# Ending the first feed-forward part in block products for all eight output tiles

## The reference

```
# first block, last step: x is 512 x 1024, hidden width 2816 = 22 x 128
h = rms_norm(x, norm_ffn_g)
x = x + (silu(h @ w_gate) * (h @ w_up)) @ w_down      # the feed-forward part
x = rms_norm(x, final_g)
# second block, first step
h = rms(x, norm_mix_g_2)
z = h @ w_in_2 + b_in_2                               # gates first, then the projections
```

## Time and profile before

| | |
|---|---|
| median of three runs | 1629.12 us |
| profiled execution | 1627.02 us |
| its span | 1625.3 us |
| PE busy | 1609.5 us, 99% |
| DVE busy | 1085.7 us, 67% |
| ACT busy | 804.6 us, 50% |
| POOL busy | 146.4 us, 9% |
| granted clock of PE, mean | 0.999 |

### The profile page before, as it was taken

The page is one execution under the profiler, slowest core; times in us unless marked ns, Lnnn a source line. Parts: engine busy times, 40 slices in busy tenths (PEclk is TensorE's granted clock), DMA queues, the critical chain, the costliest instruction groups (busy, mean ns, idle before and its releaser), DMA issues. The chain is left out here.

```text
span 1625.3 us, 23389 instructions
## 1 busy us (share of the span) xinstructions
PE 1609.5 (99%) x9266; PEld 1369.7 (84%) x9266; DVE 1085.7 (67%) x1592; ACT 804.6 (50%) x1242; POOL 146.4 (9%) x173
## 2 busy tenths in 40 slices
PE   9999999999999999999999999999999999999999
PEld 7788878888888779999999977777767888998889
DVE  5346755555573458886896896766555688867886
ACT  5344333333453347654654665256685555444453
POOL 0001001112210001000000030313111200000000
PEclk9999999999999999999999999999999999999999
DMA  8653986969756954555556749442213564363225
GB/s 297 244 184 107 246 260 189 313 245 237 222 172 216 257 139 143 182 182 176 179 186 228 246 156 237 157 160 66 66 57 125 150 201 139 117 201 107 86 90 182
DMA packets 83644, 290.32 MB, mean 179 GB/s; under 512 B 9472, under 2 KB 11648, under 8 KB 76560
## 3 DMA queue, kind: packets, MB, share of 16 engines
q1 hardware_dynamic: 76464, 238.46, 42.7%
q0 software_dynamic: 6784, 49.84, 14.5%
q10 hardware_dynamic: 288, 0.54, 0.1%
HBM read 284.58 MB, written 96.50 MB: 234 GB/s over the span
## 5 line engine op out<-in xcount | busy, mean ns | idle before, releaser
L2042 DVE TENSOR_TENSOR WL<-raw,WH 128x1024 fp32r<-128x1024 f32 (+2 forms) x358 | 420.8, 1176 | 220.1 <-ACT WH L1260 206.2
L1260 ACT ACTIVATE WH<-raw 128x1024 fp32r<-128x1024 f32 (+3 forms) x360 | 360.9, 1005 | 257.6 <-PE pst L576 251.2
L576 PE MATMUL pst<-XH,WH 128*128 128x512 f32 x960 | 385.8, 402 | 0.4 <-DVE WL L2042 0.4
L576 PE MATMUL pst<-XH,WL 128*128 128x512 f32 x960 | 374.4, 390 | 0.0
L576 PE MATMUL pst<-XL,WH 128*128 128x512 f32 x960 | 374.0, 390 | 0.0
L576 PEld LDWEIGHTS pst<-XH,WH 128*128 128x128 f32 x960 | 180.2, 188 | 48.0 <-issue 11.7
L576 PEld LDWEIGHTS pst<-XL,WH 128*128 128x128 f32 x960 | 180.4, 188 | 38.2 <-issue 2.6
L576 PEld LDWEIGHTS pst<-XH,WL 128*128 128x128 f32 x960 | 180.2, 188 | 38.3
L576 PE MATMUL pst<-TH,WH 128*128 128x256 f32 (+1 forms) x598 | 173.9, 291 | 5.6 <-DVE X L2455 4.5
L576 PE MATMUL pst<-XCH,WH 128*128 128x256 f32 x616 | 174.9, 284 | 1.2 <-ACT pst L1260 0.9
L576 PE MATMUL pst<-XCH,WL 128*128 128x256 f32 x616 | 174.4, 283 | 0.0
(11 more groups left out here) (311 smaller groups left out, 2384.3 us busy)
## 6 DMA issues: line engine op xcount, KB each, us to landing
raw<-wst SPq DMA_DIRECT2D x191, 512.0 KB, 4.2
raw<-sums SPq DMA_DIRECT2D x120, 256.0 KB, 2.9
sums<-wup POOLq DMA_DIRECT2D x8, 2816.0 KB, 36.5
sums<-sums SPq DMA_DIRECT2D x32, 704.0 KB, 6.5
sums<-wd POOLq DMA_DIRECT2D x8, 2816.0 KB, 19.7
raw<-wup SPq DMA_DIRECT2D x66, 256.0 KB, 2.9
sums<-wup SPq DMA_DIRECT2D x16, 704.0 KB, 6.2
sums<-wd SPq DMA_DIRECT2D x16, 704.0 KB, 10.3
```

The lines of the kernel that those rows point to most:

```text
L576: return nc.tensor.matmul(out, lhs, rhs, start=start, stop=stop, skip_group_check=more)
L1260: return nc.scalar.activation(out, in_, func, **kw)
L2042: vec.tensor_tensor(WL[:, i % NHL, 0:n], raw[:, i % NRAW, 0:n], WH[:, i % NHL, 0:n].bitcast(F32), ALU.subtract).then_inc(wl, 1)
```

## The change

The third part's sequence is no longer cut after 14 products: output pairs 2 and 3 get their seven products each there too, and `last` is gone on PE, ACT and DVE, with its weights. The third part then has 14 chunks of 768 columns. The even hidden tiles of the third part are stored 256 columns wide like the others. The work for finished tiles hangs on the products of the pairs 1 to 3; the last tiles are final in the order 5, 4, 7, 6. The addition of the second square is no longer the first instruction of `after1` but stands at places of its own in DVE's order. SP's load of two rows and POOL's fills, which waited for the last plain product, wait for the last block product (POOL also for the last final tile).

```
-LAST = 6
-DOWN_SEQ = {1: (MP_SEQ1, MP_SEQ1, MP_SEQ1[:14]), 2: (MP_SEQ, MP_SEQ)}
+DOWN_SEQ = {1: (MP_SEQ1, MP_SEQ1, MP_SEQ1), 2: (MP_SEQ, MP_SEQ)}
-FINAL_ORDER = ((0, 1, 3, 2, 4, 5, 6, 7), (1, 0, 3, 2, 5, 4, 7, 6))
+FINAL_ORDER = ((0, 1, 3, 2, 5, 4, 7, 6), (1, 0, 3, 2, 5, 4, 7, 6))
...
         def place(which, m):
-            return (2048 if wide(which, m) else 1792) * (m // 2 - PAIRS[which][phase(which, m)][0])
+            return 1792 * (m // 2 - PAIRS[which][phase(which, m)][0])
...
-            def last():        # PE: the 72 plain matmuls; also gone on ACT and DVE
...
-                        w = T if wide(which, m) else 256
+                        w = 256
...
-                    if ph == end and which == 2:
+                    if ph == end:
                         after(6)
                         after(7)
...
-                    if ph == end and mp and prod in ("p4", "p2" if which == 2 else "p3"):
+                    if which == 1 and ph == end and mp > 1 and prod in ("p6", "p3"):
+                        add_second(2 * mp - 3 + (0 if prod == "p6" else 1))
+                    if ph == end and mp and prod in ("p4", "p3" if which == mp == 1 else "p2"):
                         after(2 * mp - 2 + (0 if prod == "p4" else 1))
-                if ph == end and which == 2:
-                    after(6)
-                    after(7)
+                if ph == end:
+                    for n in (6, 7):
+                        if which == 1:
+                            add_second(n - 1)
+                        after(n)
...
             def after1(n):
                 m = FINAL_ORDER[0][n]
-                if n > 1:
-                    add_second(n - 1)
                 dve.wait_ge(*final(1, m))
...
-            pool.wait_ge(mm_, DONE["ffn_last", 7])
+            pool.wait_ge(mm_, DONE["ffn_down1", len(DOWN[1]) - 1])
+            pool.wait_ge(*final(1, FINAL_ORDER[0][7]))
...
-            sp.wait_ge(mm_, DONE["ffn_last", 7])
+            sp.wait_ge(mm_, DONE["ffn_down1", len(DOWN[1]) - 1])
```

More of the change, by code:

```diff
@@ L97, in ffn @@
             up, down = up + a, down + b
-        if n == 1:
-            plan.extend(("ffn_last", i) for i in range(4 * LAST // CH))
     take("v", 4), take("q", 4), take("k", 4)
@@ L135, in main_counts @@
             tile[name, "gate", 2 * (i // 3) + i % 3] = n
[L136 to L142, removed]
         elif name in DOUBLE:
@@ L525, in phase @@
             return [ph for ph, t in enumerate(TILES[which]) if m in t][0]
-        def wide(which, m):
-            return which == 1 and phase(which, m) == 2
         def place(which, m):
-            return (2048 if wide(which, m) else 1792) * (m // 2 - PAIRS[which][phase(which, m)][0])
+            return 1792 * (m // 2 - PAIRS[which][phase(which, m)][0])
         def span(which, m, slot, n=1):
-            a = place(which, m) + 256 * (slot + (wide(which, m) and slot > 0))
+            a = place(which, m) + 256 * slot
             return slice(a, a + 256 * n)
@@ L982, in down @@
                 at["ring"] = 2
-            def last():
[L985 to L1002, removed]
             def ffn(which):
@@ L1010, in ffn @@
                     down(which, ph)
-                if which == 1:
-                    last()
             ffn(1)
@@ L2595, in dve_program @@
             at["ring"] = 2
-            last()
+            add_second(7)
             def bank2():
```

2 lines of the change are left out of this document (removed).

## The result

The changed kernel takes 1637.67 us (median of 4 runs, 1636.51 to 1638.19) against 1628.72 for the kernel before, measured beside it (4 runs, 1627.27 to 1629.22): 1.0056 of the time, 95% interval 1.0041 to 1.0071, so 9 us slower. 1636.6 was forecast, in a range from 1631 to 1640. The profiled execution took 1638.16 us, its span is 1636.4.

What follows compares the result with a forecast made beforehand. DVE, full at the seam between block and plain products, was taken to bound the stage: its bill, hand-overs and POOL start the sums of squares at 986.9 instead of 979.40, 7.5 us later, giving 1636.6 us by the median, range 1631 to 1640.

Steps and rivals of the forecast that it cites:

- PE's bill: PE's matmuls at the seam: 72 of 512 columns removed, 126 of 256 added, 16.3 against 15.1 us, 1.2 saved.
- the wait at (1, p4): PE's wait before block product (1, p4), for a DVE addition out of PSUM: to fall from 2.1 to 1.9 us.
- DVE's bill: DVE's conversions and additions before the sums of squares: 12.2 us added, 5.8 removed, 0.27 less for splits, net 6.1.
- The two hand-overs at chunks 12 and 13: DVE idle 1.6 us, twice, while ACT writes the second square, whose one buffer DVE had to free, and converts.
- the wait before (3, p6): PE standing still before block product (3, p6), for DVE's conversion of chunk 13: some 3.9 us.
- the third hand-over: Wait of about 1.1 us at chunk 11, whose ACT conversion needs chunk 8's buffer and so PE's product (2, p5).
- POOL, the term that was mis-sized: POOL's seven additions of first squares slow DVE instructions beside them: 0.6 us each taken, bounds nothing and 1.05.
- the lower clock inside the stage: PE at 1.2 GHz after its waits of 1.9 and 3.9 us; without it the sums would start at 985.6, not 986.9.
- the walk: Row-by-row schedule through the queues of PE, DVE and ACT: sums of squares start at 986.9 instead of 979.40.
- The clock behind the sums: PE at half its clock after its wait of 2.4 to 2.9 us for the sums, 1.6 us on top.
- My likeliest case: The forecast 1636.6 us, with the end of the stage 5.5 to 8.5 us later; chance 0.48.
- rival 3: The wait for the sums, 2.4 to 2.9 us, also lowers PE's clock, 1.6 us on top: 1638.2; chance 0.22.

Runs made afterwards that it cites:

- buffer and no POOL: Changed kernel with a second buffer for the second squares and without POOL's seven additions of first squares: 1.7 us below the kernel before, ratio 0.9978 to 0.9996.
- before with the same and more left out: Kernel before the change with a second buffer for second squares, without additions of squares on POOL and DVE: 0.5 us below the kernel before, ratio 0.9988 to 1.0006.
- The dummy load: Kernel before the change with eight more DVE multiplications of 128 x 512 that nobody reads: 4.8 us above the kernel before, ratio 1.0020 to 1.0045.

## Why the prediction was right

- **DVE, not PE, sets the end of the stage.** Shown: relieving DVE turns the loss into a gain, and loading it by 7.2 us makes a loss of the same kind without the change (3.8 us of stretch).
- **PE's bill, 1.2 us less.** The two kernels with room on DVE whose clock fell alike (buffer and no POOL; before with the same and more left out) differ by 0.6 in the stretch. Less the 0.25 by which the wait at (1, p4) is shorter, and with 0.8 us of small new waits that the sum did not have, PE's own saving is some 1.1.
- **DVE's bill, 6.1 us, of which 1.8 were spare.** The dummy load agrees (3.8 against 3.9 expected), with the reserve that it cost more than its estimate. The pages show the bill more directly: with the additions of squares left out on POOL and DVE, DVE's busy time over the span is 1076.6 us in the kernel before and 1082.5 in the changed one, 5.9 more. The spare time was larger than I read it. PE starts the sums when the first of the two splits is done, 0.74 us after they begin (986.73 and 987.47), and not when both are, so the kernel before had 2.3 us.
- **The two hand-overs at chunks 12 and 13.** At their place and of their size, 1.52 against 1.6; the wait before (3, p6) is 4.16 against 3.9. I named a DVE conversion as its releaser; it ended 0.3 us before an ACT copy in the same jam. The wait before (2, p4) is 1.25, not 0.6, those before (3, p5) and (3, p4) did not come. Nor did the third hand-over of 1.1 us, at chunk 11: from 944 DVE stands still nowhere before 962.43.
- **POOL, the term that was mis-sized.** I put 0.6 us on each addition, 2.0 in all on the path (984.9 to 986.9), and 1.05 each as the upper bound, 3.9. Each cost 0.82 on the average, and the seven 4.5 us at the split, more than that bound. The Trainium skill, SBUF — State Buffer, section "Who interferes with whom", has the instruction that comes second wait out the first. The trace agrees: each delay is what was left of POOL's addition, to 0.14 us. I had read that rule as POOL's whole length.
- **That the sum held is luck.** I had counted 1.3 us for the lower clock inside the stage, and in that execution the clock held behind the first wait, and its fall behind the wait at (3, p6) lay under DVE's queue. Without POOL and clock the walk said 983.1; the kernel without POOL's additions starts its sums at 982.1. On the same footing the walk gave POOL 2.5 us (983.1 to 985.6), and it took 4.5. So POOL was 2.0 too low, the clock 1.3 and the rest 1.0 too high: 986.6 beside the 986.9 of the forecast. The totals show the same. The splits end 9.5 us later than before by the same scale, where 9.4 were forecast. But 7.4 of them are busy time of DVE (36.78 us from 947.52 to 988.01, against 29.38), where the bill had 6.1, and 2.1 are idle time, where I had 3.4. Of the 1.3 us more of busy time 1.0 is POOL's: it held up DVE by 5.8 us here and by 4.8 in the kernel before.
- **The clock behind the sums.** My likeliest case left it out and gave it 0.22. It came: the sums started 7.2 late (7.5 forecast), and 1.4 went behind them. That is the step that failed, and most of the 1.1 us by which the time lies above the forecast. What came is rival 3's case, whose 1638.2 is nearer to 1637.67 than my 1636.6. The Trainium skill, TensorE: Matmul & The Clock Gate, section "HAM oscillation — how this bites in real kernels", tells of waits longer than these 2.56 us that are charged twice; here this one was.

## What to carry to other kernels

Fewer matmul columns are worth something only where the engine that empties PSUM has room: count the reading engine's instructions for the stage of the change, not for the span (DVE was busy 67% of the span and 19.92 of 20 us here). When two engines hand a buffer to and fro, look at what is queued right behind the waiting instruction on both; one more buffer took 4.2 us off the stretch. And a helper engine's work isn't free to a full engine beside it: here seven additions cost 5.0 us of the stretch on POOL and 3.7 on DVE itself, by one trace each.

## What the runs showed of the hardware that was not expected

- The granted clock falls to 0.50 (1.2 GHz) behind an idle time of about 1.9 us in some executions and not in others, at the same place. Behind the wait before (1, p4), 1.83 to 1.85 us long in nine of these kernels, it fell in four and held in five; in the three kernels with plain products, where it is 2.10 to 2.11 us, it fell in all three; behind the wait of 1.9 us near 1220 it fell in six of twelve. Each fall costs up to 1.6 us. Runs of one kernel differ by some 3 us, so a fall or two may be most of that; this isn't shown. I can't tell from these traces what decides it.
- POOL and DVE wait for each other, but only in some instructions. DVE's that were too long in the changed kernel have both inputs in SBUF; additions from PSUM beside the same POOL instruction kept their 0.41. Each of the seven was held up by what POOL's instruction had left, less 0.13 to 0.14 us. POOL is held up in the same way. Its shortest addition takes 1.28 us. The one of 1.70 began at 958.05, while DVE's conversions had 0.56 left (to 958.61), and is 0.42 longer (DVE's rows around POOL's):

```profile
956.80 1.81 DVE L1993 TENSOR_TENSOR WL<-raw,WH 128x768 fp32r<-128x768 f32 x2
958.05 1.70 POOL L3001 TENSOR_TENSOR acc<-acc,misc 128x512 f32<-128x512 f32 x1 [3.45 <-ACT misc L1224]
958.54 0.41 DVE L2406 TENSOR_TENSOR X<-X,pst 128x256 f32<-128x256 f32 x1
```
